# Two transformer blocks on one core: query projections drawn forward in the second attention, weight splits moved in three stages

## The reference

```python
def mla_attention(h, w_in, q_norm_g, kv_norm_g, w_uq, w_ukv, w_o, cos, sin):
    proj = h @ w_in
    c_q = rms_norm(proj[..., :MLA_Q_RANK], q_norm_g)
    ...
    q = (c_q @ w_uq).reshape(b, s, MLA_HEADS, MLA_NOPE + MLA_ROPE)
    ...
        sc = (jnp.einsum('bqhd,bkhd->bhqk', qn, k_nope)
              + jnp.einsum('bqhr,bkr->bhqk', qp, k_pe)).astype(jnp.float32) * scale
        p = masked_softmax(sc, chunk_mask_2(blk, s)[None, None])
        return jnp.einsum('bhqk,bkhe->bqhe', p.astype(v.dtype), v)
    ...
    return o.reshape(b, s, MLA_HEADS * MLA_V) @ w_o

def second_block(x, ...):
    for i in range(DEPTH_2):
        h = rms_norm(x, attn_norm_g[i])
        x = x + (diff_attention(...) if i == 0 else mla_attention(...))
        h = rms_norm(x, ffn_norm_g[i])
        x = x + conv_ffn(h, ffn_w_up[i], ffn_conv_w[i], ffn_conv_b[i], ffn_w_down[i])
    return rms_norm(x, final_norm_g)
```

## Time and profile before

| | |
|---|---|
| median of 3 runs | 1051.89 us (1051.37 to 1051.95) |
| profiled execution | 1052.46 us, span of its instructions 1050.7 us |
| PE | busy 1028.6 us, 98% of the span |
| DVE | busy 729.9 us, 69% |
| ACT | busy 572.0 us, 54% |
| TensorE's granted clock | 0.997 of full speed on average |
| attention loop of the second layer | 776 to 831 us |
| output projection and its stage | 831 to 856.4 us |

### The profile page before, as it was taken

How to read it: one execution, slowest core, us unless ns; L and a number is a source line. 1 busy time by engine, 2 the same in 40 slices (tenths; PEclk the granted TensorE clock), 3 DMA queues, 4 the chain that set the end, 5 groups by cost and what they waited for, 6 DMA issues and landing times.

```text
span 1050.7 us, 19999 instructions
## 1 busy us (share of the span) xinstructions
PE 1028.6 (98%) x7892; PEld 990.1 (94%) x7892; DVE 729.9 (69%) x969; ACT 572.0 (54%) x795; POOL 6.6 (1%) x20
## 2 busy tenths in 40 slices
PE   7999999999999999999999999999999989999997
PEld 6999999999999999978899999999989989999996
DVE  6676654558665456777878777777876577777775
ACT  6555566545443443567866555554637464555554
POOL 0000000000000000000000000000020000000000
PEclk9999999999999999999999999999999999999999
DMA  8636565455655644453555666663434374666651
GB/s 292 205 124 197 180 200 196 160 182 179 214 187 196 203 160 166 158 198 121 168 153 159 203 180 180 180 180 111 136 71 120 113 212 139 190 189 189 188 159 75
DMA packets 191266, 178.89 MB, mean 170 GB/s; under 512 B 17444, under 2 KB 169586, under 8 KB 191218
## 3 DMA queue, kind: packets, MB, share of 16 engines
q1 hardware_dynamic: 191218, 178.22, 54.6%
HBM read 177.15 MB, written 1.05 MB: 170 GB/s over the span
## 4 chain that ended last, share of the span: by engine, by line
PE 89%; DVE 5%; ACT 3%; DMA 2%; issue 1%; SPq 0%; DVEq 0%; ACTq 0%
PE psum L609 24%; PE psum L611 24%; PE psum L610 24%; PE psum L616 4%; PE psum L617 4%; PE psum L618 4%; DVE whl L1707 2%; ACT whl L1221 1%; PE psum L950 1%; PE psum L934 1%; PE psum L949 1%; ACT prob L1462 1%; DMA x_rows<-x 1%; DMA raw<-da_w_qkv 0%; DVE stat L2084 0%
## 5 line engine op out<-in xcount | busy, mean ns | idle before, releaser
L609 PE MATMUL psum<-hT,whl 128*128 128x256 f32 x1392 | 395.9, 284 | 4.3 <-DVE hT L1782 4.3
L611 PE MATMUL psum<-hT,whl 128*128 128x256 f32 x1392 | 394.4, 283 | 0.0
L610 PE MATMUL psum<-hT,whl 128*128 128x256 f32 x1392 | 394.3, 283 | 0.0
L1707 DVE TENSOR_TENSOR whl<-raw,whl 128x2048 fp32r<-128x2048 f32 (+2 forms) x145 | 298.3, 2063 | 92.1 <-ACT whl L1221 91.8
L1221 ACT ACTIVATE whl<-raw 128x2048 fp32r<-128x2048 f32 (+2 forms) x145 | 248.7, 1717 | 113.0 <-DMA raw<-w_ff 67.9
L609 PEld LDWEIGHTS psum<-hT,whl 128*128 128x128 f32 x1392 | 267.3, 192 | 6.0 <-DVE hT L1782 4.2
L610 PEld LDWEIGHTS psum<-hT,whl 128*128 128x128 f32 x1392 | 267.3, 192 | 0.9
L611 PEld LDWEIGHTS psum<-hT,whl 128*128 128x128 f32 x1392 | 267.3, 192 | 0.0
L609 PE MATMUL psum<-lat,whl 128*128 128x256 f32 (+1 forms) x512 | 145.8, 285 | 0.0
L610 PE MATMUL psum<-lat,whl 128*128 128x256 f32 (+1 forms) x512 | 144.7, 283 | 0.0
L611 PE MATMUL psum<-lat,whl 128*128 128x256 f32 (+1 forms) x512 | 144.7, 283 | 0.0
(11 more groups left out here) (246 smaller groups left out, 1386.7 us busy)
## 6 DMA issues: line engine op xcount, KB each, us to landing
raw<-w_ff SPq DMA_DIRECT2D x32, 1024.0 KB, 5.5
raw<-w_in SPq DMA_DIRECT2D x24, 1024.0 KB, 5.2
raw<-ffn_w_up SPq DMA_DIRECT2D x44, 512.0 KB, 5.0
q_sb<-ffn_w_up SPq DMA_DIRECT2D x44, 512.0 KB, 5.0
raw<-da_w_qkv SPq DMA_DIRECT2D x12, 1024.0 KB, 5.2
q_sb<-ffn_w_down SPq DMA_DIRECT2D x22, 512.0 KB, 3.6
raw<-ffn_w_down SPq DMA_DIRECT2D x22, 512.0 KB, 3.6
raw<-w_proj_a SPq DMA_DIRECT2D x4, 1024.0 KB, 5.2
```

Of the source, the lines that this page charges most:

```text
L609: mm(dst, weight(n, 0, cols, kt, c0, m), hi, start=start, stop=False, skip_group_check=True)
L610: mm(dst, weight(n, 0, cols, kt, c0, m), lo, start=False, stop=False, skip_group_check=True)
L611: return mm(dst, weight(n, 1, cols, kt, c0, m), hi, start=False, stop=stop, skip_group_check=True)
L1707: tt(whl[:, slot, 1, 0:w], landing(n)[:, 0:w], whl[:, slot, 0, 0:w].bitcast(F32), ALU.subtract).then_inc(lo_ready, 1)
```

## The change

It moves instructions, adds none and takes none away. On the PE of the second attention, four query projections stand before the second scores instead of two (queries 0, 1, scores 0, queries 2, 3), and from then on the query of pair c+2 comes behind the scores of pair c-1. Of the eight rows of blocks of the output projection's first chunk, one is put into step 6, two into step 7, and one stays behind the loop. On DVE the lower splits of this loop are written one chunk further ahead (N_UQ+c+3 in step c). In the square stage of this projection ACT's upper splits are one chunk further ahead (`split_hi(N_WO2+3)` before the first quarter), and DVE's first lower split stands before the first sum. In the first attention the mean of x is taken 24 matmuls later. At the end of the feed-forward before the second attention ACT's next upper split stands before the last `Silu`.

```diff
@@ -1005,11 +1005,10 @@
             turn_rows(0, 0)
             rows(1, 0, (1,))
             turn_rows(0, 1)
-            rows(1, 1, (0,))
+            rows(1, 1)
+            rows(2, 0, (0,))
             pe.wait_ge(std_ready, sum(SUMS[:QKV]) + 1)
             mean(QKV, 1)
-            rows(1, 1, (1,))
-            rows(2, 0, (0,))
             turn_rows(1, 0)
             rows(2, 0, (1,))
             turn_rows(1, 1)
@@ -1176,19 +1175,30 @@
 
             pe.wait_ge(k_read, 8)
             pe.wait_ge(lat_ready, 5)
-            for c in range(9):
-                proj, sc, tn, wt, ot = [lag <= c < 8 + lag for lag in range(5)]
-                if proj:
-                    project(N_UQ + c, lat, kts=Q_RANK // P)
-                if sc:
-                    mla_scores(c - 1)
+            def query(p):
+                project(N_UQ + p, lat, kts=Q_RANK // P)
+
+            query(0)
+            query(1)
+            mla_scores(0)
+            query(2)
+            query(3)
+            for c in range(2, 9):
+                _, _, tn, wt, ot = [lag <= c < 8 + lag for lag in range(5)]
+                mla_scores(c - 1)
+                if c + 2 < 8:
+                    query(c + 2)
                 if wt:
                     mla_weigh(c - 3)
                 if ot:
                     mla_outputs(c - 4)
+                if c == 6:
+                    part(N_WO2, range(0, 1))
+                if c == 7:
+                    part(N_WO2, range(1, 3))
                 if tn:
                     mla_turn(c - 2)
-            part(N_WO2, range(0, 4))
+            part(N_WO2, range(3, 4))
             mla_weigh(6)
             mla_outputs(5)
             mla_turn(7)
@@ -1357,16 +1367,13 @@
 
             def square_stage(n0, gain, lead=LEAD):
 
-                if lead == LEAD:
-                    split_hi(n0 + LEAD)
+                split_hi(n0 + lead)
                 for c in range(4):
                     n = n0 + c
                     act.wait_ge(bank_free[n % RING], uses(n) + 1)
                     round_x(c, gain)
                     square_x(c)
-                    if lead > LEAD:
-                        split_hi(n + lead)
-                    elif c < 3:
+                    if c < 3:
                         split_hi(n + 1 + lead)
 
             def ffn(l, n0, units, k, gain=None):
@@ -1393,8 +1400,7 @@
                             ins = fn(conv_out[:, q, b, :], conv_in[:, q, b, 2:], ACT.Identity, bias=conv(3, b, j),
                                      scale=conv(2, b, j))
                         ins.then_inc(f["conv_b"], 1)
-                        if not last:
-                            split(0)
+                        split(0)
                         act.wait_ge(f["conv_g"], j + 1)
                         fn(t_act[:, q, 0, :], conv_out[:, q, 0, :], ACT.Silu).then_inc(f["silu"], 1)
                     act.wait_ge(f["z_f"], j + 1)
@@ -1405,8 +1411,6 @@
                         fn(zT[:, q, :, 0, :], t_dve[:, q, :, :], ACT.Copy).then_inc(f["z_hi"], 1)
                     else:
                         fn(zT[:, q, late, 0, :], t_dve[:, q, 0, :], ACT.Copy).then_inc(f["z_hi"], 1)
-                        if last:
-                            split(0)
                         split(1)
 
                 if k != FFN1:
@@ -1542,9 +1546,9 @@
             take_columns(0, 1)
             split_hi(n + 3)
             take_rows(1, 0)
-            deviation(QKV, 1)
             take_rows(1, 1)
             split_hi(n + 4)
+            deviation(QKV, 1)
             take_columns(1, 0)
             take_columns(1, 1)
             split_hi(n + 5)
@@ -1645,6 +1649,7 @@
                     fn(v_sb[:, t, c * 512:(c + 1) * 512].rearrange("p (a b) -> p a b", a=2), up[t][:],
                        ACT.Copy, scale=r_tok[:, TT + t:TT + t + 1]).then_inc(v_read, 1)
             split_hi(N_UQ + LEAD)
+            split_hi(N_UQ + LEAD + 1)
 
             def pair_turned_out(p):
@@ -1659,7 +1664,7 @@
                     exponentials(c - 1, DA_HEADS + c - 1, up)
                 if tn:
                     take_turned(DA_HEADS + c - 2, 2)
-                if c < 8:
+                if 0 < c < 8:
                     split_hi(N_UQ + c + LEAD + 1)
             pair_turned_out(5)
             take_turned(DA_HEADS + 7, 2)
@@ -1936,6 +1941,8 @@
 
             def square_stage(n0, k, gain, lead=LEAD):
 
+                if lead > LEAD:
+                    split_lo(n0 + lead)
                 for c in range(4):
                     n = n0 + c
                     chunk_wait(n)
@@ -1946,7 +1953,7 @@
                     rest_x(k, c, gain)
                     if c > 0:
                         add_pair(k, c)
-                    if c < 3 and lead > LEAD:
+                    if 0 < c < 3 and lead > LEAD:
                         split_lo(n + lead)
                 tt(ss[:, 0, :], ss[:, 0, :], ss[:, 1, :], ALU.add).then_inc(ss_ready, 1)
                 split_lo(n0 + 3 + lead)
@@ -2132,8 +2139,8 @@
             split_lo(n + 3)
             rope(1, 0)
             rope(1, 1)
+            split_lo(n + 4)
             step.wait(step.mark(reciprocal_deviation(QKV, 1)))
-            split_lo(n + 4)
             normalise_x()
             split_lo(n + 5)
             pair_max(0)
@@ -2247,8 +2254,6 @@
                         step.wait(step.mark(nc.vector.reciprocal(rstd[:, 0, :], std[:, 0, :])))
                         step.wait(step.mark(stt(scaled[:], rstd[:, 0, :], MLA_SCALE, cos_mla, ALU.mult, ALU.mult)))
 
-            split_lo(N_UQ + LEAD)
-
             def pair_outputs(p):
 
                 q = p % 4
@@ -2264,24 +2269,33 @@
                 dve.wait_ge(o_hi, 4 + p + 1)
                 tt(mT[:, p, 1, :], out_bank(p)[:, p % 2, :], mT[:, p, 0, :].bitcast(F32), ALU.subtract).then_inc(om_ready, 1)
 
-            for c in range(9):
-                proj, sc, _, wt, ot = [lag <= c < 8 + lag for lag in range(5)]
-                if proj:
-                    n = N_UQ + c
-                    chunk_wait(n)
-                    tt(q_sb[:, 2 * c:2 * c + 2, :], bank[bank_of(n)], over_blocks(scaled[:]),
-                       ALU.mult).then_inc(bank_free[bank_of(n)], 1)
-                if sc:
+            def take_query(p):
+
+                n = N_UQ + p
+                chunk_wait(n)
+                tt(q_sb[:, 2 * p:2 * p + 2, :], bank[bank_of(n)], over_blocks(scaled[:]),
+                   ALU.mult).then_inc(bank_free[bank_of(n)], 1)
+
+            take_query(0)
+            split_lo(N_UQ + LEAD)
+            take_query(1)
+            split_lo(N_UQ + LEAD + 1)
+            for c in range(1, 9):
+                if c > 1:
                     pair_max(DA_HEADS + c - 1)
-                    if c < 8:
-                        split_lo(N_UQ + c + LEAD)
-                if wt:
+                else:
+                    pair_max(DA_HEADS)
+                    take_query(2)
+                if c + 2 < 8:
+                    take_query(c + 2)
+                if c < 8:
+                    split_lo(N_UQ + c + LEAD + 1)
+                if c >= 3:
                     pair_outputs(c - 3)
-                if ot:
+                if c >= 4:
                     pair_rest(c - 4)
             pair_outputs(6)
             pair_rest(5)
-            split_lo(N_WO2 + LEAD)
             pair_outputs(7)
             pair_rest(6)
             pair_rest(7)
```

## The result

| | before | after |
|---|---|---|
| median | 1051.63 us (1051.33 to 1051.95, 4 runs) | 1071.80 us (1071.64 to 1074.37, 4 runs) |
| ratio to before | | 1.0193, 95% interval 1.0179 to 1.0207 |
| profiled execution | 1052.46 us | 1074.37 us |
| PE busy | 1028.6 us | 1038.6 us |
| mean granted clock, profiled execution | 0.997 | 0.986 |

The change costs 20 us. The profiled execution of after was the slowest of its four. The other three took 1071.64 to 1071.87 us at a mean clock of 0.989 to 0.990.

A forecast was written before the change was run, and what follows sets the result against it. TensorE, busy 98% of the span, was taken as the bound; 1052.46 + 19.2 + 2.4 - 5.4 - 0.8 - 0.3 = 1067.6, less 0.57 for the median gave 1067.0 us. Own range 1065 to 1069, overall 1060.5 to 1071.

The forecast's parts named there:

- the ring: Second attention's loop: DVE, ACT and PE wait on each other in turn, 8.37 us a step, 9.09 from c=5.
- the walk: Second attention's loop traced from the first query, each operation taking the later of its engine and its signal; 23.5 us waits.
- +19.2: Second attention's loop: PE waits of 23.5 us together in place of 4.3, so 19.2 us lost.
- the rings are looser: Rival, second attention's loop: 0.1 us less at each of nine hand-overs in five rings, -4.5, 1062.5 us; chance 0.09.
- The expected growth of DVE's waits: Second attention's loop: DVE's `whl` led by waits on ACT, 1.6 us growing to 5.4, some 24 us in all.
- The clock: Half clock after three loop waits near 4 us: 1.65 us each, 4.95 in all, some 2.5 hidden, +2.4 us.
- The clock holds: Rival: the clock does not fall at the loop's three long waits, 1064.6 us; chance 0.14.
- The clock stays low: Rival: half clock throughout 816 to 843, weights-times-values and output transposes 1.5 us more each ring, about +3, 1070; chance 0.1.
- The faster case: Rival: upper splits are ready when DVE reaches them in steps 3 to 7, so waits go, about 1043 us; chance 0.05.
- 2 to 3 us, if nothing else happened: Second attention's loop: forward queries and output projection pieces fill the 1.21 and 1.52 us waits on `prob`, giving back 2 to 3.
- The square stage: Square projection: the PE's wait on `hT` (3.7 us by starts) and the slow clock behind it (1.65) go, -5.4 us.
- The small edits: First attention: wait for the sum of squares goes, -0.8 us; feed-forward before the second attention: earlier upper split, -0.3 us.

The follow-up runs named there:

- the filled kernel: After, with seven unused float32 matmuls ahead of weights-times-values 3, 4 and 5 in the second attention's loop: 1065.89 us, ratio 1.0135.
- only the last wait filled: After, with the seven unused matmuls ahead of weights-times-values 5 alone: 1070.36 us, ratio 1.0173.
- the loop alone: The kernel before with only the second attention's loop changed as in after: 1077.51 us, ratio 1.0246 to before.
- the ring cut at ACT: After, with ACT's upper split moved from the end to the start of each loop step from the second on: 1049.34 us, ratio 0.9979 to before.

## Why the prediction was right, and where it was wrong

**The direction and the ring: right.** With DVE one chunk ahead of ACT, every step became a ring through all three queues. The predicted starts of the lower splits, moved by the 1.85 us that the first query came earlier, are 785.25, 790.85, 797.85, 806.15, 815.65, 824.65 and 833.95. The trace has 785.09, 790.77, 797.76, 806.19, 815.69, then 827.07 and 838.70. Up to the first fall of the clock the walk is within 0.16 us; so is the first long wait's end (818.58; 815.65 with the predicted 2.20, 0.20 and 0.48 gives 818.53). With the clock held by fillers, the loop took 73.5 us from the first query (773.56) to its end (847.08), where it took 53.8 before (776.11 to 829.92): 19.7 us more, and +19.2 was predicted. So the waits, most of the loss, were sized right, and "the rings are looser" is ruled out. The expected growth of DVE's waits from 1.6 to 5.4 us holds up to the first fall (5.34); the two behind it, 6.84 and 7.10, are the slow clock's, since with fillers they are 4.69 and 4.88.

**The clock: the step that failed.** The median, 1071.8 us, is 4.8 above the forecast and 0.8 above the stated range. The prediction charged 1.65 us for each of three falls and took 2.5 of these 4.95 us as hidden in waits that follow, +2.4 in all. Two things were wrong in it. First, the length: I took the 3.4 us of the earlier trace rows for each, and the clock stayed low for 6.8, 6.8 and 13.7 us. Second, the cover. The waits that follow are ends of the same ring, and the ring runs through the matmuls that slowed down, so they moved along instead of shrinking. ACT's rows of that ring show it:

```profile
821.87 0.38 ACT L1657 ACTIVATE mT<-psum 128x256 fp32r<-128x256 f32 x1 [6.21 <-PE psum L1162]
...
824.43 0.81 ACT L1482 ACTIVATE attnT<-psum 128x768 f32<-128x768 f32 x1 [0.57 <-PE psum L934]
825.14 1.90 ACT L1231 ACTIVATE whl<-raw 128x2048 fp32r<-128x2048 f32 x1
```

From weights-times-values (818.58) to `mT` there are 3.29 us instead of 1.29 + 0.42 = 1.71. From `mT` to `attnT` there are 2.56 instead of 0.28 + 1.60 = 1.88, since the transposes of the probabilities, also at half clock, were not done. That is 2.26 us more, and the ring from 818.58 to 829.96 took 11.38 us against 9.09, or 9.23 in the filled kernel. The next took 11.64 us, filled 9.42. The third fall covers dense work: 15.53 us from 841.60 to the loop's end, filled 10.54. Together the clock cost 9.4 us in the profiled execution, 7.0 more than charged, and the loop ended 27.2 us later where 19 to 22 were expected. With the measured terms in place of the predicted ones, 1052.46 + 19.7 + 9.4 - 5.3 for the square stage - 1.85 for the earlier first query is the measured 1074.4.

In the medians the falls cost less: 6.1 us or somewhat more by the filler experiment. Three traces of this loop show why. Against the 73.5 us of the filled one it took 4.6 us more with 13.6 us at half clock (only the last wait filled), 6.6 more with 20.5 (the loop alone) and 9.4 more with 27.3 (after). So each time about a third of the time at half clock was lost, and the three other executions of after, at a mean clock of 0.989 to 0.990 against 0.986, spent less time there. Why the falls of one and the same loop last longer in one execution than in another, no run shows.

**The rivals.** "The clock holds" fell. "The clock stays low" was the case nearest to the truth. It named the right place (weights-times-values and output transposes on the ring, 1.5 us each; measured 1.58) but left out the probabilities' transposes (0.7) and the dense end (5.0), and I gave it a tenth. The faster case fell where the prediction said it would be decided, at the first split of 2048 columns, which waited 5.34 us. The chip confirms that point from the other side: with the upper split ahead of `attnT` the kernel is 0.2% faster than before.

**The gain that was asked for.** "2 to 3 us, if nothing else happened" was not tested by itself. With the ring cut at ACT the waits before the second and third scores are gone, but 1.52, 1.52 and 0.82 us stand before the fifth to seventh, and the loop is slower than the old one. Whether the forward queries are worth anything under a better order of ACT (with `mT` behind `attnT` too, for one) is open.

**The square stage: right.** -5.4 us predicted. The loop's end is 27.2 us later in the profiled execution and the end of the span 21.9 us later, so 5.3 us came back behind the loop. By itself on the chip the edit gave 5.8 us.

**The small edits: right.** The first query comes 1.85 us earlier. Of that 0.76 us were there before the first attention, where nothing had changed yet, and 1.09 are the edits'; predicted were 0.8 + 0.3. By the starts behind each of them, the first attention gave 0.84 and the end of the feed-forward 0.2. No timing here can tell so little from nothing.

## What to carry to other kernels

When work is split over queues that run in order, count for each producer and consumer who is how many items ahead. A consumer that asks one item early for what its producer makes last in the step ties all queues into one ring, whose length is the sum of the parts and not their maximum; walk that ring by starts, since such a walk held to 0.2 us here up to the first fall of the clock and to 0.5 us over the loop. Then price a slow clock as part of the ring: if slowed matmuls lie on it, nothing hides their cost, and a wait that is expected to swallow it only moves along. Where waits near 4 us can't be removed at once, some matmuls put into them can hold the clock; here that gave back 6 of 20 us.

## What the runs showed of the hardware

How long the clock stays low differs, also between executions of one loop. After a wait of 3.34 us and dense work it was 3.4 us (the kernel before). In after it fell during the waits of 3.73 and 4.14 us, when the PE had stood idle for 2.9 and 2.1 us, and came back after 6.8 us each time, in the middle of work without a gap. After the third wait, of 4.26 us, it stayed low for 13.7 us, though the PE was busy 96% of the time. In the same loop with the rest of the kernel as before, the three falls lasted 3.4, 6.8 and 10.2 us. With fillers of 3.19 us in those waits the trace has no fall, with gaps of 0.7 to 0.9 us left, nor has any of these traces one at the waits of 1.5 to 1.7 us. In the loop a fall cost about a third of its length. At half clock a weights-times-values matmul pair started every 0.43 us instead of 0.22.
